# Narrow score matmuls in layer C, and feed-forward up products with both halves of the activation side by side

## The reference

```python
def conv_ffn(u, w_up, conv_w, conv_b, w_down):          # D_FF = 2816
    hdn = causal_dwconv(u @ w_up, conv_w) + conv_b       # 3 taps along the tokens
    gate, val = jnp.split(hdn, 2, axis=-1)
    return (jax.nn.silu(gate) * val) @ w_down
...
# HGRN2, 8 heads of 128: attn[l, s] = sum_d q[l,d] * exp(G[l,d] - G[s,d]) * k[s,d], for s <= l
diff = G_[..., :, None, :] - G_[..., None, :, :]
pair_decay = jnp.exp(jnp.where(incl, diff, -jnp.inf))
attn = jnp.einsum("bhld,bhlsd,bhsd->bhls", q_, pair_decay, k_)
```

## Time and profile before

| | us |
|---|---|
| median of 3 runs | 1141.88 (1140.98 to 1142.22) |
| profiled execution, whole | 1141.13 |
| its span | 1139.7 |
| PE busy | 1028.4 (90%) |
| DVE busy | 721.4 (63%) |
| ACT busy | 611.5 (54%) |
| POOL busy | 65.8 (6%) |

### The profile page before, as it was taken

One profiled execution on the slowest core, in us unless ns is written; L12 is line 12 of the kernel. 1 busy time (PEld: TensorE's weight loads), 2 busy tenths in 40 slices (PEclk: granted clock), 3 DMA queues, 4 the chain that ended last, 5 costly groups with the idle time before them and its releaser, 6 DMA issues.

```text
span 1139.7 us, 16015 instructions
## 1 busy us (share of the span) xinstructions
PE 1028.4 (90%) x6496; PEld 918.4 (81%) x6496; DVE 721.4 (63%) x1067; ACT 611.5 (54%) x944; POOL 65.8 (6%) x44
## 2 busy tenths in 40 slices
PE   7999888998888899998699999969999669999995
PEld 5777668976667798887699999959988659999995
DVE  5775657455554676665677667656675557677665
ACT  5564745345447554454755555575324465555554
POOL 0000000000000014300000000000433000000000
PEclk9999999999889899998899999979999889999998
DMA  8643344542132432322355555526434144655650
GB/s 294 210 129 109 113 129 149 184 129 74 56 117 87 130 109 77 93 91 95 111 172 197 181 187 188 185 75 190 145 110 130 59 145 148 199 174 186 197 171 37
DMA packets 43546, 158.49 MB, mean 139 GB/s; under 512 B 4944, under 2 KB 5328, under 8 KB 43344
## 3 DMA queue, kind: packets, MB, share of 16 engines
q1 hardware_dynamic: 42608, 154.70, 42.5%
q0 software_dynamic: 576, 2.10, 0.5%
q10 hardware_dynamic: 288, 0.67, 0.2%
HBM read 156.40 MB, written 1.05 MB: 138 GB/s over the span
## 4 chain that ended last, share of the span: by engine, by line
PE 74%; DVE 12%; ACT 11%; issue 1%; DMA 0%; SPq 0%; ACTq 0%; DVEq 0%
PE psum L386 72%; DVE w_lo L372 3%; ACT w_hi L363 2%; PE psum L395 2%; ACT u_hi L569 1%; DVE u_lo L580 1%; DVE scr L1445 1%; DVE feat L1705 1%; ACT scr L1405 1%; DVE scr L1453 1%; DVE scr L1456 1%; DVE scr L2578 1%; ACT normed L484 1%; DVE x_res L674 1%; ACT normed L516 1%
## 5 line engine op out<-in xcount | busy, mean ns | idle before, releaser
L372 DVE TENSOR_TENSOR w_lo<-raw,w_hi 128x1024 fp32r<-128x1024 f32 x288 | 358.1, 1253 | 203.6 <-ACT w_hi L363 203.3
L363 ACT ACTIVATE w_hi<-raw 128x1024 fp32r<-128x1024 f32 x288 | 303.3, 1055 | 187.0 <-PE psum L386 182.9
L386 PE MATMUL psum<-u_hi,w_hi 128*128 128x256 f32 x1088 | 312.1, 287 | 0.6 <-DVE u_lo L580 0.3
L386 PE MATMUL psum<-u_lo,w_hi 128*128 128x256 f32 x1088 | 310.1, 285 | 0.0
L386 PE MATMUL psum<-u_hi,w_lo 128*128 128x256 f32 x1088 | 310.0, 285 | 0.0
L386 PEld LDWEIGHTS psum<-u_hi,w_hi 128*128 128x128 f32 x1088 | 211.4, 194 | 3.3 <-DVE u_lo L580 1.1
L386 PEld LDWEIGHTS psum<-u_lo,w_hi 128*128 128x128 f32 x1088 | 211.2, 194 | 1.8 <-issue 0.2
L386 PEld LDWEIGHTS psum<-u_hi,w_lo 128*128 128x128 f32 x1088 | 211.0, 194 | 0.0
L386 PE MATMUL psum<-w_hi,u_hi 128*128 128x512 f32 x432 | 178.1, 412 | 13.6 <-DVE u_lo L580 7.8
L386 PE MATMUL psum<-w_lo,u_hi 128*128 128x512 f32 x432 | 171.2, 396 | 0.0
L386 PE MATMUL psum<-w_hi,u_lo 128*128 128x512 f32 x432 | 171.2, 396 | 0.0
(11 more groups left out here) (267 smaller groups left out, 1105.1 us busy)
## 6 DMA issues: line engine op xcount, KB each, us to landing
raw<-in_pieces SPq DMA_DIRECT2D x288, 512.0 KB, 3.5
feat<-in_norm_gains POOLq DMA_DIRECT2D x4, 512.0 KB, 4.1
const<-in_table SPq DMA_DIRECT2D x1, 1408.0 KB, 8.3
out_x<-x_res SPq DMA_DIRECT2D x1, 1024.0 KB, 4.0
x_res<-in_x ACTq DMA_DIRECT2D x1, 512.0 KB, 5.0
x_res<-in_x SPq DMA_DIRECT2D x1, 512.0 KB, 4.8
cols<-in_cols SPq DMA_DIRECT2D x1, 380.0 KB, 4.1
par<-in_par SPq DMA_DIRECT2D x1, 203.0 KB, 7.1
```

Of the source, the lines that this page charges most:

```text
L363: act.q.activation(w_hi[i % SPLIT][:, :], raw[i % RAW][:, :], ACT.Copy).then_inc(act.done, act.mark("hi", i))
L372: dve.q.tensor_tensor(w_lo[i % SPLIT][:, :], raw[i % RAW][:, :], w_hi[i % SPLIT][:, :].bitcast(F32), ALU.subtract).then_inc(dve.done, dve. ...
L386: return pe.q.matmul(o, lhs, rhs, start=start, stop=stop, **kw)
```

## The change

**Feed-forward.** u_hi and u_lo of this block now lie side by side in one buffer, `u_both` (8 x 2 x 256). For each slice the hi weights meet both at once, one matmul of 512 columns into a whole PSUM bank, and the lo weights meet u_hi alone, 256 columns into the first half of the bank. Gate and value now have a bank each, two tiles four banks. The two halves of a bank still have to be added: ACT copies the first halves to `up_sum`, DVE adds the second halves, and the three taps read `up_sum` in SBUF. The steps of a tile are spread over two rounds of ACT's and DVE's loops, and PE issues up(j), then down(j-2) (`FFN_LAG = 2` puts the weight pieces in that order).

**Layer C.** Each score matmul has 32 weight columns and writes 32 PSUM partitions: 32 matmuls for a group's diagonal (32 moving columns), 32 for a level with n < 32 (16 moving columns), 16 for n = 32 (32 columns) and 16 for n = 64 (64 columns). Blocks off the level's own are no longer written. The diagonal is kept by a predicated copy into a buffer that POOL has set to zero.

```diff
@@ -120,7 +120,7 @@
 
 
 N_PAR = _par()
-FFN_LAG = 1
+FFN_LAG = 2
...
+    u_both = over_scr("u_both", SCR - 4096, KT, 2, S)
+    u_f = (u_both[:, :, 0, :], u_both[:, :, 1, :])
     conv = [view(scr, i * 512, 2, S) for i in range(2)]
     silu = [view(scr, 1024 + i * S, S) for i in range(2)]
     prod = [view(scr, 1536 + i * S, S) for i in range(2)]
+    up_sum = [view(scr, 4096 + i * 512, 2, S) for i in range(2)]
...
             pe.wait_ge(dve, f"n{l}2", "lo", 2 * part + 1)
             if j >= 2:
-                pe.wait_ge(dve, "conv", l, j - 2)
+                pe.wait_ge(dve, "up_sum", l, j - 2)
             else:
-                for step in evicted(f"mix{l}", 0):
-                    pe.wait_ge(*step)
+                for c in range(2):
+                    for step in evicted(f"mix{l}", c):
+                        pe.wait_ge(*step)
             for i in range(2):
                 for kk in range(KT // 2):
-                    k = part * KT // 2 + kk
-                    last = mm3(psum[:, j % 2, i * S:(i + 1) * S], (hi[:, i, kk, :], lo[:, i, kk, :]),
-                               [u[:, k, :] for u in u_t], (i, k) == (0, 0), k == KT - 1)
+                    k, bank = part * KT // 2 + kk, 2 * (j % 2) + i
+                    mm(psum[:, bank, :], hi[:, i, kk, :], u_both[:, k, :, :].rearrange("p a s -> p (a s)"), k == 0,
+                       False, True)
+                    last = mm(psum[:, bank, 0:S], lo[:, i, kk, :], u_f[0][:, k, :], False, k == KT - 1, True)
...
     def act_up(l, j):
-        act_hi()
-        act_hi()
+        bank = 2 * (j % 2)
         act.wait_ge(pe, "up", l, j)
...
-            act.wait_ge(dve, "hid", l, j - 2)
+            act.wait_ge(dve, "conv", l, j - 2)
+        act.q.activation(up_sum[j % 2], psum[:, bank:bank + 2, 0:S], ACT.Copy).then_inc(act.done, act.mark("up", l, j))
+
+    def dve_up_sum(l, j):
+        bank = 2 * (j % 2)
+        dve.wait_ge(act, "up", l, j)
+        dve.q.tensor_tensor(up_sum[j % 2], psum[:, bank:bank + 2, S:2 * S], up_sum[j % 2], ALU.add).then_inc(
+            dve.done, dve.mark("up_sum", l, j))
...
+    def act_taps(l, j):
+        act.wait_ge(dve, "up_sum", l, j)
+        if j >= 2:
+            act.wait_ge(dve, "prod", l, j - 2)
         for i in range(2):
-            last = act.q.activation(conv[j % 2][:, i, :], psum[:, j % 2, i * S:(i + 1) * S], ACT.Identity,
+            last = act.q.activation(conv[j % 2][:, i, :], up_sum[j % 2][:, i, :], ACT.Identity,
                                     scale=col(f"tap2_{l}", j + i * FT), bias=col(f"bias_{l}", j + i * FT))
         last.then_inc(act.done, act.mark("tap2", l, j))
...
+    def dve_taps(l, j):
         dve.wait_ge(act, "tap2", l, j)
         for tap in (1, 0):
...
-                dve.q.scalar_tensor_tensor(conv[j % 2][:, i, back:], psum[:, j % 2, i * S:(i + 1) * S - back],
+                dve.q.scalar_tensor_tensor(conv[j % 2][:, i, back:], up_sum[j % 2][:, i, 0:S - back],
                                            col(f"tap{tap}_{l}", j + i * FT), conv[j % 2][:, i, back:], ALU.mult,
                                            ALU.add).then_inc(dve.done, dve.mark(f"tap{tap}", l, j, i))
...
-    def act_gated(l, j):
...
+    def act_silu(l, j):
         act.wait_ge(dve, "conv", l, j)
+        if j >= 2:
+            act.wait_ge(dve, "prod", l, j - 2)
         act.q.activation(silu[j % 2], conv[j % 2][:, 0, :], ACT.Silu).then_inc(act.done, act.mark("silu", l, j))
...
+    def dve_prod(l, j):
+        dve.wait_ge(act, "silu", l, j)
+        if j >= 2:
+            dve.wait_ge(dve, "hid", l, j - 2)
+        dve.q.tensor_tensor(prod[j % 2], silu[j % 2], conv[j % 2][:, 1, :], ALU.mult).then_inc(
+            dve.done, dve.mark("prod", l, j))
...
+    def act_hid(l, j):
         act.wait_ge(dve, "prod", l, j)
...
     def pe_ffn(l, free):
         pe_norm(f"n{l}2", free)
-        for j in range(FT):
-            pe_up(l, j)
+        for j in range(FT + 2):
+            if j < FT:
+                pe_up(l, j)
+            if j >= 2:
+                pe_down(l, j - 2)
+
+    def act_ffn(l, x):
+        act_norm(f"n{l}2", [(u_f, gain_of(f"n{l}2"))], (x, "x"))
+        for j in range(FT + 1):
+            if j < FT:
+                act_hi()
+                act_hi()
+                act_up(l, j)
             if j >= 1:
-                pe_down(l, j - 1)
-        pe_down(l, FT - 1)
-
-    def act_ffn(l, x):
-        act_norm(f"n{l}2", [(u_t, gain_of(f"n{l}2"))], (x, "x"))
-        for j in range(FT):
-            act_up(l, j)
+                act_silu(l, j - 1)
+            if j >= 2:
+                act_hi()
+            if j < FT:
+                act_taps(l, j)
             if j >= 1:
-                act_hi()
-            act_gated(l, j)
+                act_hid(l, j - 1)
...
+        for j in range(FT + 1):
+            if j < FT:
+                dve_lo()
+                dve_lo()
+                dve_up_sum(l, j)
             if j >= 1:
+                dve_prod(l, j - 1)
+            if j >= 2:
                 dve_lo()
-            dve_gated(l, j)
+            if j < FT:
+                dve_taps(l, j)
+            if j >= 1:
+                dve_hid(l, j - 1)
...
         for j in range(8):
             h = 4 * g + j // 2
-            last = mm(psum[:, 2 + 2 * g + j // 4, (j % 4) * P:(j % 4 + 1) * P], ck[:, h, blk(j)], cq[:, h, blk(j)])
+            for lo in range(0, P, 32):
+                at = (j % 2) * P + lo
+                last = mm(psum[lo:lo + 32, 2 + 2 * g + j // 4, (j % 4) * P + lo:(j % 4) * P + lo + 32],
+                          ck[:, h, at:at + 32], cq[:, h, at:at + 32], loose=True)
         last.then_inc(pe.done, pe.mark("C.diag", g))
...
             at = GB * g + P * j
-            last = mm(psum[:, b, 64 * j:64 * j + 64].rearrange("p (b n) -> p b n", n=n), kd_f[:, at:at + P],
-                      qd[:, at:at + P].rearrange("p (b two n) -> p b two n", two=2, n=n)[:, :, 1, :])
+            if n < 32:
+                for lo in range(0, P, 32):
+                    last = mm(psum[lo:lo + 32, b, 64 * j + lo // 2:64 * j + lo // 2 + 16].rearrange(
+                        "p (b n) -> p b n", n=n), kd_f[:, at + lo:at + lo + 32],
+                        qd[:, at + lo:at + lo + 32].rearrange("p (b two n) -> p b two n", two=2, n=n)[:, :, 1, :],
+                        loose=True)
+            else:
+                for lo in range(0, P, 2 * n):
+                    for r in range(lo, lo + n, 32):
+                        last = mm(psum[r:r + 32, b, 64 * j + lo // 2:64 * j + lo // 2 + n], kd_f[:, at + r:at + r + 32],
+                                  qd[:, at + lo + n:at + lo + 2 * n], loose=True)
...
-            free = [(dve, "conv", 0, FT - 2), (dve, "conv", 0, FT - 1)] if c < 2 else c_evicted(c - 2)
+            free = [(dve, "up_sum", 0, FT - 2), (dve, "up_sum", 0, FT - 1)] if c < 2 else c_evicted(c - 2)
...
     def dve_c_diag(g):
         dve.wait_ge(pe, "C.diag", g)
-        dve.q.tensor_tensor(group_att(g), bank_heads(2 + 2 * g, 2), ident.unsqueeze(1).broadcast_to([P, 8, P]),
-                            ALU.mult).then_inc(dve.done, dve.mark("C.diag", g))
+        dve.wait_ge(pool, "C.att0")
+        dve.q.copy_predicated(group_att(g), ident.bitcast(I32).unsqueeze(1).broadcast_to([P, 8, P]),
+                              bank_heads(2 + 2 * g, 2)).then_inc(dve.done, dve.mark("C.diag", g))
...
     def pool_c():
+        pool.wait_ge(dve, "n10", "lo", 0)
+        pool.q.memset(att, 0.0).then_inc(pool.done, pool.mark("C.att0"))
         pool.wait_ge(dve, "C.gate", 0)
```

More of the change, by code:

```diff
@@ L2558, in act_up @@
     def act_up(l, j):
-        act_hi()
-        act_hi()
+        bank = 2 * (j % 2)
         act.wait_ge(pe, "up", l, j)
         if j >= 2:
-            act.wait_ge(dve, "hid", l, j - 2)
+            act.wait_ge(dve, "conv", l, j - 2)
[9 more added lines that the diff above has]
+            act.wait_ge(dve, "prod", l, j - 2)
         for i in range(2):
-            last = act.q.activation(conv[j % 2][:, i, :], psum[:, j % 2, i * S:(i + 1) * S], ACT.Identity,
+            last = act.q.activation(conv[j % 2][:, i, :], up_sum[j % 2][:, i, :], ACT.Identity,
                                     scale=col(f"tap2_{l}", j + i * FT), bias=col(f"bias_{l}", j + i * FT))
         last.then_inc(act.done, act.mark("tap2", l, j))
-    def dve_up(l, j):
-        dve_lo()
-        dve_lo()
+    def dve_taps(l, j):
         dve.wait_ge(act, "tap2", l, j)
@@ L2589, in act_gated, with dve_hid @@
         act.q.activation(hid[j % 2][0][:, :], prod[j % 2], ACT.Copy).then_inc(act.done, act.mark("hid", l, j))
-    def dve_gated(l, j):
-        dve.wait_ge(act, "silu", l, j)
-        dve.q.tensor_tensor(prod[j % 2], silu[j % 2], conv[j % 2][:, 1, :], ALU.mult).then_inc(
-            dve.done, dve.mark("prod", l, j))
+    def dve_hid(l, j):
         dve.wait_ge(act, "hid", l, j)
@@ L2627, in dve_ffn @@
     def dve_ffn(l):
-        dve_norm(f"n{l}2", [(u_t, gain_of(f"n{l}2"))])
-        for j in range(FT):
```

(11 more changed lines are left out.)

## The result

The changed kernel takes 1126.8 us (median; 1121.6 to 1128.0), the kernel before 1142.05 (1141.0 to 1145.1): ratio 0.9865, 95% interval 0.9846 to 0.9883. The profiled execution took 1127.98 us, its span 1126.7.

A forecast was written before the change was run, and what follows sets the result against it. The prediction took TensorE's (PE's) issue to bound the kernel. Against the profiled 1141.13 us it summed -8.4 (feed-forward steady state), +3.1 (its ends) and +1.5 (layer C) to -3.8, 1137.3, so a median of 1138.1, range 1130 to 1154.

The forecast's parts named there:

- the price of a narrow pair: Layer C's score matmuls: 0.032 us for each of 832 pairs, 0.056 for each of 64 at n = 64.
- lower bound: Layer C: tiles run side by side, pairs at 0.016 and 0.028 us, 15.1 us in all, -13.6.
- rival 3: Layer C: column tiles run side by side, C -13.6, time 1123 us; chance 0.08.
- Rival 2: Layer C: changing tile width empties the array, about 0.4 us there and back, 15 trips, +6.2, 1144.3 us; chance 0.08.
- a gap of 0.2 at each edge: Layer C: sign in the trace that a change of tile width empties the array.
- The forecast +1.5: Layer C's score matmuls as a whole: 30.2 us after the change against 28.7 before.
- rival 1: Layer C: narrow pairs cost what instructions cost, not columns; at 0.056 us a pair +21.5, 1158.1 us; chance 0.30.
- At no cost: Layer C: DVE's predicated diagonal copies, 2.0 us each, twice, and POOL's memset add no time.
- Feed-forward, steady state: Both feed-forward blocks: 0.19 us less per tile from wide matmuls at 0.228, 44 tiles, -8.4 us.
- my own alternative of 0.235: Feed-forward steady state: wide matmuls at 0.235 us would leave a gain of only -3.5 us.
- Its ends: Start and end of the feed-forward blocks: longer PE waits for split weights and hid, +3.1 us (0 to +6).
- rival 4: Feed-forward: the lag is not long enough, DVE turns late in each tile, all 8.4 lost, 1146.5 us; chance 0.04.

The follow-up runs named there:

- same_tile: The changed kernel with layer C's narrow score matmuls reordered, all eight of one column tile before the next tile's: 1139.05 us, ratio 0.9988 to the kernel before.
- tile64: The changed kernel with the ten n < 32 score blocks in two column tiles of 64 weight columns, 32 moving, instead of four of 32: 1128.76 us.
- gates_f32: The changed kernel with layer AB's 24 gate matmuls (16 weight columns) fed as f32 instead of fp32r: 1123.73 us in one run.
- pairs2: The changed kernel with both groups' score blocks of a level adjacent, two quarters behind them, and q(1) scaled ahead of the diagonal copy: 1131.75 us.
- c_only: The kernel before with layer C's part of the change alone, feed-forward as before: 1127.39 us, ratio 0.9896.
- up_grouped: The changed kernel with four wide up matmuls issued, then four narrow ones, instead of in turn: 1124.46 us, ratio 0.9857 to the kernel before.
- best: The changed kernel with q(1) scaled ahead of the diagonal copy and up matmuls in runs of four wide, four narrow: 1122.41 us, ratio 0.9836 to before.

## Why the prediction was wrong

**The step that failed: the price of a narrow pair.** I took 0.032 for each of 832, one behind the other. The 0.032 was the right price within a tile (0.031 to 0.032 in same_tile; 0.58 over 16 pairs a tile, 0.036, in the change), and the reason I gave, the load at 0.9 ns a column, is borne out by tile64. What failed is that pairs of four different column tiles follow each other here, and run side by side: 0.0091 a pair. For n = 64 it was the same: 0.056 a pair holds within a tile (0.89 over 16 pairs, the 54 ns of 64 moving columns), but two tiles share the time, and the block takes 1.02 us for the 1.8 forecast. The section held side by side as its lower bound and as rival 3, at 0.08. I set it aside since "all pairs share the 128 rows"; the 64-row tiles of the earlier trace rows had shown two tiles side by side, and nothing in the rows said that columns were different. That the bound, -13.6, is also the sum of the measured terms below is luck: it took pairs at 0.016, two side by side, and no price for a trip. The Trainium skill (TensorEngine Tiling (Array Packing), Key Properties) lists that different tiles can load weights and multiply in parallel; the trace agrees, 64 pairs in 0.58. TensorE: Matmul & The Clock Gate, Part 3 of the Trainium skill, says that a load overlaps running matmuls only where the row group differs. All pairs here use all 128 rows, so by that load and stream would take turns, 64 x (0.028 + 0.014) = 2.7 us by the prices of the prediction; the block took 1.83 in same_tile and 0.67 in the change, so the rule holds here neither within a column tile nor between them.

**Rival 2 was true as well.** I gave a trip into narrow tiles 0.4 (15 of them are 6.0, not the 6.2 written) and a chance of 0.08. It costs 0.28, 15 times, 4.2 us, though not as the sign "a gap of 0.2 at each edge" had it: 0.09 of it stands at the entry. The argument against it, the 16-column loads of the earlier trace rows with no gap, was taken from fp32r matmuls, and gates_f32 shows that in f32 the same shapes have one. The rivals were written as if one excluded the other, though both could hold. Layer C, priced with what was measured: 12 blocks x 0.58 + 2 x 0.50 (n = 32) + 2 x 0.89 (n = 64; both read as the second of two adjacent blocks in pairs2) + 15 x 0.28 = 13.9 us for 28.7, -14.8; waits +0.8 and +0.4; -13.6. The stretch gave 13.1 (and 13.2 in c_only). The forecast +1.5 is off by 15 us, and that is all of the error and more.

**The floor for small matmuls** (rival 1, chance 0.30) did not bind: starts in different tiles stand 9 ns apart on the mean. Within a tile they stand 31 ns apart or more, about what the load takes; whether a floor holds there no run shows.

**DVE in layer C.** "At no cost" was nearly right: 1.35 us a copy, not 2.0, and the one place where I said it could show is the one where it did, as a wait of 0.84, because PE now arrives early. The two short waits on evictions come from the shorter steps too.

**Feed-forward, steady state:** forecast -8.4, measured 44 x (8.387 - 8.50) = -5.0. The term was mis-sized: 0.2358 for the wide matmul, not 0.228. The rows showed "0.23" and my own alternative of 0.235 (-3.5) was the nearer one; I had taken 0.228 from down matmuls, which differ from these by neither rows nor columns. Part of the difference is the order (up_grouped), the rest is open; and since the same down matmuls took 0.2289 in the change and 0.2306 in up_grouped (2.747 and 2.767 over 12), their price is not theirs alone.

**Its ends:** forecast +3.1, measured +1.2: 1.0 for 1.5 ahead of the first down (0.6 before), and 2.5 for 2.9 ahead of the last but one, with no wait after it, as foreseen (2.5 and 2.0 before). The half clock of 3.4 us behind one of these waits moved from the first block to the second; the kernel after shows it here, and not at 748:

```profile
1110.40:1113.80 3.40, 3.40 (x10) 2.62 (x9) 0.42 (x1) 1.49 (x2) 0.00 (x0) 0.50 0.00 0
```

That is why feed-forward 0 gave 3.7 and feed-forward 1 nothing; each is some 1.9 without it. In the second block this is no chance of one execution: all ten traces of kernels with the new feed-forward and its wide and narrow matmuls in turn show it there; the kernel before and c_only do not, nor do up_grouped and best, whose wait is 2.4 us. What decides it is open. In the first block it comes and goes. The prediction had left the clock as it was, with -1.7 to +1.7 for it. The lag of two tiles was long enough (rival 4 falls): no wait inside either block.

**Sum by measured terms:** -5.0 + 1.2 - 13.6 = -17.4, and +3.8 of layers A and B in this one execution: -13.6, against 1127.98 - 1141.13 = -13.2.

## What to carry to other kernels

Matmuls on a quarter of the columns are worth it when neighbours in the queue use different column tiles: put the tile in the innermost loop. Price them per tile, by the load or by the stream, whichever is longer (0.028 and 0.054 us for 32 weight columns and 64 moving ones), and divide by the tiles; then add the edge to the neighbours of full width once per trip. Where a stage of PE shrinks, look at what DVE had done just in time: here a swap of two DVE operations took away a wait of 0.84 us, and merging blocks to save edges cost more cover than edges.
